# Attention stage of a hybrid diffusion step: one of two GpSimd folds taken out, VectorE adds both halves, and ScalarE writes the first copy of the running sum

## The reference, cut to what matters

```python
def one_block(qi):
    s = jnp.einsum('bqhgd,bkhd->bhgqk', qi.astype(F32), k.astype(F32))
    p = jax.nn.softmax(s, axis=-1)
    return jnp.einsum('bhgqk,bkhd->bqhgd', p, v.astype(F32))
```

## Time and profile before

| | |
|---|---|
| median of 3 runs | 3383.89 us (3378.5 to 3384.28) |
| profiled execution, its own time | 3377.92 us |
| its span, first to last instruction | 3376.2 us |
| attention stage in it (exponentials) | 282.4 to 1079.8 us |
| mean granted TensorE clock | 0.971 of full speed |

### The profile page before, as it was taken

How to read it: one execution, slowest core, us unless ns; L and a number is a source line. 1 busy time by engine, 2 the same in 40 slices (tenths; PEclk the granted TensorE clock), 3 DMA queues, 4 the chain that set the end, 5 groups by cost and what they waited for, 6 DMA issues and landing times. The chain is left out here.

```text
span 3376.2 us, 48426 instructions
## 1 busy us (share of the span) xinstructions
PE 3177.5 (94%) x18066; PEld 2778.3 (82%) x18066; DVE 2378.0 (70%) x3262; ACT 1713.6 (51%) x2475; POOL 1710.5 (51%) x910
## 2 busy tenths in 40 slices
PE   6988999999998799998899699999999999899998
PEld 5975777777776797887688699999999999688886
DVE  4877999999996575339633588988888987222367
ACT  5865888888887685221244433344444333211122
POOL 2655999999997011111023377756766774000001
PEclk8998999999998899999999899999999999899999
DMA  6432011111100444338575567757785775555466
GB/s 217 156 121 76 28 49 45 51 44 47 49 21 24 141 154 144 109 97 260 174 226 183 184 202 229 238 163 245 230 246 156 225 221 158 191 200 183 175 254 224
DMA packets 431529, 518.42 MB, mean 154 GB/s; under 512 B 40112, under 2 KB 322048, under 8 KB 431296
## 3 DMA queue, kind: packets, MB, share of 16 engines
q1 hardware_dynamic: 384224, 412.21, 38.4%
q10 hardware_dynamic: 43968, 91.86, 7.9%
q0 software_dynamic: 3104, 11.27, 0.8%
HBM read 341.62 MB, written 173.64 MB: 153 GB/s over the span
## 5 line engine op out<-in xcount | busy, mean ns | idle before, releaser
L781 POOL TENSOR_TENSOR att_tlo<-att_prob,att_thi 128x1024 fp32r<-128x1024 f32 x292 | 694.0, 2405 | 62.7 <-ACT att_thi L950 62.7
L166 PE MATMUL fu_p<-fu_hhi,fu_whi 128*128 128x384 f32 x1848 | 619.5, 335 | 28.5 <-PEq L111 18.5
L168 PE MATMUL fu_p<-fu_hhi,fu_wlo 128*128 128x384 f32 x1848 | 618.6, 335 | 0.0
L167 PE MATMUL fu_p<-fu_hlo,fu_whi 128*128 128x384 f32 x1848 | 618.5, 335 | 0.0
L945 ACT ACTIVATE att_prob<-att_p_s 128x512 f32<-128x512 f32 x584 | 341.4, 592 | 86.7 <-PE att_p_s L841 80.8
L166 PEld LDWEIGHTS fu_p<-fu_hhi,fu_whi 128*128 128x128 f32 x1848 | 348.0, 188 | 31.5 <-issue 18.8
L993 DVE TENSOR_REDUCE att_mx<-att_p_r 128x1 f32<-128x512 f32 x512 | 341.4, 683 | 44.4 <-PE att_p_r L805 43.3
L167 PEld LDWEIGHTS fu_p<-fu_hlo,fu_whi 128*128 128x128 f32 x1848 | 347.9, 188 | 0.0
L168 PEld LDWEIGHTS fu_p<-fu_hhi,fu_wlo 128*128 128x128 f32 x1848 | 347.8, 188 | 0.0
L950 ACT ACTIVATE att_thi<-att_prob 128x1024 fp32r<-128x1024 f32 x292 | 309.8, 1061 | 9.3
L1807 POOL TENSOR_TENSOR fu_wsum<-fu_ws 128x1024 f32<-128x1024 f32 x66 | 178.7, 2708 | 233.9 <-DMA fu_ws<-in_w_ffn_dram 124.1
(11 more groups left out here) (361 smaller groups left out, 8045.0 us busy)
## 6 DMA issues: line engine op xcount, KB each, us to landing
fu_ws<-in_w_ffn_dram SPq DMA_DIRECT2D x132, 512.0 KB, 8.3
gated_d<-fu_out SPq DMA_DIRECT2D x99, 448.0 KB, 5.8
fd_src<-gated_d SPq DMA_DIRECT2D x63, 704.0 KB, 4.2
second_d<-fu_hs ACTq DMA_DIRECT2D x77, 512.0 KB, 3.3
fu_hs<-in_w_ffn_dram ACTq DMA_DIRECT2D x121, 256.0 KB, 4.2
fd_second<-second_d SPq DMA_DIRECT2D x40, 512.0 KB, 5.9
fd_w<-second_d SPq DMA_DIRECT2D x37, 512.0 KB, 5.3
ga_h<-hT_d SPq DMA_DIRECT2D x36, 512.0 KB, 4.2
```

What stands on the lines that cost most here:

```text
L166: pe.matmul(out, ah, bh, start=first, stop=False)
L167: pe.matmul(out, ah, bl, start=False, stop=False)
L168: return pe.matmul(out, al, bh, start=False, stop=last)
L781: pool.tensor_tensor(tlo[:, sl, :], prob[:, sl, :], thi[:, sl, :].bitcast(F32), ALU.subtract).then_inc(s.lo, 1)
```

## The change

Step 6 leaves the list of folded steps. POOL has one fold less in each latent unit, and DVE adds both halves of step 6. The copy of the first half into `p_sum` goes from DVE to ACT, in step 1, right behind ACT's copy of the finished sum; it waits for that copy (`sums_out`), and DVE's next addition waits for it (`s.sum`).

```diff
     AHEAD = 2
-    FOLDED = (2, 6)
+    FOLDED = (2,)
...
                         act.activation(sums[:, b.kv, :], p_sum[:, :], ACT.Copy).then_inc(s.sums_out, 1)
+                    if S.sum and S.sum[1] == 0:
+                        b, j = S.sum
+                        act.wait_ge(s.ex, b.g0 * 2 + 1)
+                        wait(act, s.sums_out, b.n)
+                        act.activation(p_sum[:, :], prob[:, b.step_no[0] % SLOTS_P, 0:ROW], ACT.Copy).then_inc(s.sum, 1)
                     if S.fin:
...
-                    if i == 0 and j == 0:
-                        wait(dve, s.sums_out, b.n)
-                        dve.tensor_copy(p_sum[:, :], half).then_inc(s.sum, 1)
-                    else:
-                        dve.wait_ge(s.sum, done)
-                        dve.tensor_tensor(p_sum[:, :], p_sum[:, :], half, ALU.add).then_inc(s.sum, 1)
+                    dve.wait_ge(s.sum, done)
+                    dve.tensor_tensor(p_sum[:, :], p_sum[:, :], half, ALU.add).then_inc(s.sum, 1)
...
                         for i in range(1 if b.nds > 1 and j in FOLDED else 2):
-                            add(b, j, i)
+                            if i or j:
+                                add(b, j, i)
                             if pieces:
                                 piece(*pieces.pop(0))
```

## The result

The changed kernel takes 3397.21 us (median of 12 runs, 3391.79 to 3404.0), the one before 3382.89 us (12 runs, 3376.32 to 3390.19). The ratio is 1.0049, with a 95% interval of 1.0041 to 1.0057: slower by half a per cent, with POOL relieved of a fold in each unit. The profiled execution has a span of 3390.0 us against 3376.2.

A forecast was written before the change was run, and what follows sets the result against it. The bound was taken to be a ring of waits, PE, ACT up to `osb`, DVE, PE, not full POOL. 31 x 0.41 = 12.7 us plus 0.3 us made 13.0 us, so about 3397 us; range 3383 to 3406.

The forecast's parts named there:

- the ring PE, ACT up to `osb`, DVE, PE: Attention stage: three engines carry each unit in turn, each waiting for the one before; POOL is full but bounds nobody.
- both gates: Values DVE's long stretch needs, `osb` and the fold of step 2; forecast 0.35 us late by `osb`, 0.41 with the fold.
- The fold taken from POOL: Step 6: frees 1.26 us of POOL a unit, worth 0 on the ring; bounds 0 and 1.26 us.
- the rival that POOL is the bound: Whole stage: it would lose what POOL loses, 32 x 1.26 = 40 us, giving 3344 us; chance 12%.
- The copy taken from DVE in step 1: Step 1 on DVE: frees 0.60 us, worth 0 as the next maximum waits for PE anyway; bounds 0 and 0.60.
- The third addition of step 6: Three DVE additions in a row: next maximum 0.08 us late, covered by idle time, cost 0; uncovered 0.80 us a unit.
- The copy on ACT: Step 1 on ACT: delays the exponentials, `osb` and the fold, so DVE's long stretch starts 0.41 us late each unit.
- The second gate: Fold of step 2, late through `thi` of step 1: raises the delay of DVE's long stretch from 0.35 to 0.41 us.
- The sum: 31 latent units x 0.41 = 12.7 us, with 0.3 us for the first and prompt units: 13.0 us, about 3397 us.
- The prompt part: The four prompt units, priced together with the first unit: 0.3 us for the copy's move, bounds 0 and 3 us.
- the short wait for the fold: Sign in the changed profile: the reader of the fold in step 2 may show a short wait for POOL.
- The sign for the third addition: Sign in the changed profile: maximum behind the three additions comes no later from the unit's first score than before.

The follow-up runs named there:

- e1: Kernel before with only the fold of step 6 taken out, the first copy staying on DVE: 3378.2 us, ratio 0.999.
- e2: Changed kernel with both folds kept (steps 2 and 6), so only the copy moves from DVE to ACT: 3401.55 us, ratio 1.0059.
- e3: Kernel before with ACT's `osb` moved in front of `thi` of step 2: 3373.93 us, ratio 0.9984 to before.
- e4: Changed kernel with ACT's `osb` moved in front of `thi` of step 2: 3394.52 us, ratio 1.0041 to before.
- e9: Changed kernel with one DVE maximum ahead of the addition of the fold, `osb` left behind `thi`: 3395.9 us, ratio 1.0048 to before.
- e6: Kernel before with `osb` early, one DVE maximum ahead of the fold's addition, and step 6 unfolded: 3355.1 us, ratio 0.992.
- e5: Kernel before with `osb` early and one DVE maximum ahead of the fold's addition, both folds kept: 3361.5 us, ratio 0.9942.
- e8: Kernel before with a third fold on POOL, in step 4: 3416.67 us, ratio 1.0103.
- e7: Changed kernel with `osb` early and one DVE maximum ahead of the fold's addition: 3375.47 us, ratio 0.9982 to before.

## Why the prediction was right

*The bound.* The reading that POOL's 98% bounds nobody, and that the ring PE, ACT up to `osb`, DVE, PE does, was right for the latent units but the last: e1 shows the first half, e2, e3, e4 and e9 the second. One wait was left out of the ring: PE's piece also waits for the reciprocal behind `osb` (in 400 to 1000 us 22.1 us at its weight load, 11.9 before). It does not set the pace, since in e4 it is gone and the unit is the same. The rule of highest occupancy (the Trainium skill, "Perfetto Trace Analysis", "Identifying the Most-Contended Engine") named POOL. e1 does not bear that out in 30 of the 32 latent units; at the end of the stage the fold less gave 3 us of the 40 that the rule would have made of it. With both gates open, e6 against e5, it gave 0.21 us a unit, a sixth of the 1.26 us.

*The fold taken from POOL*, put at 0: 0 in each of the 30 units (24.38 us in e1), but 1.55 us less in the last latent unit and 1.55 us less in the first prompt unit, where the prediction had not looked. There the rival that POOL is the bound had a point.

*The copy taken from DVE in step 1*, put at 0: the maximum behind it still waits for PE (0.47 us idle in the changed kernel where the copy stood), and DVE's idle time before L1040 grew. This agrees, though no run takes the copy from DVE and leaves ACT as it was.

*The third addition of step 6*, put at 0.08 us late and covered: 0.02 us late in e1. Right.

*The copy on ACT*, the term that counted, was right in its path and too small in size. I had it start 0.61 us behind the copy of `sums` and hold the next for 0.48; it started 0.67 us behind (883.99 to 884.66) and held it for 0.54 (to 885.20), 0.06 us more at each end. The exponentials of step 1 come 0.74 us late instead of 0.61, `osb` 0.47 instead of 0.35, the fold's addition 0.51 instead of 0.41, and the unit is 0.53 us longer instead of 0.41. The second gate, the fold, is real: in the changed kernel it adds about 0.05 us (the addition starts 0.15 us behind the reciprocal's start, 0.10 before) to 0.08 us (e9), where 0.06 had been put (0.41 - 0.35).

*The sum.* 30 units gave 15.9 us where 31 x 0.41 = 12.7 had been put. The last latent unit gave 0.95 us back, for which the prediction had nothing: the copy alone makes it 0.56 us longer (e2, 25.01 us), the fold less alone 1.55 us shorter (e1). The prompt part, from its first score to the end of the stage, took 0.3 us more (33.58 to 33.88), as put, but by luck: 2.47 us more in e2 and 1.55 us less in e1. The profiled execution starts the stage's scores 2.2 us earlier than the one of before and spends 2.3 us more on the first unit (28.15 against 25.85). e8, which has neither half of the change, has a first unit of 28.19 us too, and e9, which has both, one of 26.49, so this is not the change's. In the end 3397.21 us against 3397, with the medians 14.3 us apart and the ratio at 16.6 us (0.0049 x 3383): 13.0 us had been put for what measured 14.3 to 16.6. The agreement to the microsecond is luck: the 30 units were priced 3.2 us too low in all and the copy at the end of the stage too low as well, the fold's 3 us there were left out, and the median of before fell by 1.0 us with more runs (3383.89 to 3382.89).

*The signs.* DVE's idle time before L1040, 1 us or more: 1.15. The wait in step 2 on ACT gone: yes. POOL's share down by 5 points: 6.8, and its waits for `thi` more and longer (84 instead of 37, up to 1.5 us instead of 0.3). A wait for the copy itself at DVE's addition, which would have spoken against the prediction, is not in the list of 400 to 1000 us; nor is the short wait for the fold that I had thought possible. The sign for the third addition was badly put: I wrote that the maximum behind it would come no later from the first score, but it lies behind the delayed stretch and comes 23.47 us after it (904.03 - 880.56) instead of 22.91. That is the unit's own 0.53 us, as e1 shows by its absence.

## What to carry to other kernels

Before moving work off a full engine, look for who waits for it: here an engine that was 98% busy with an empty list of waiters had nothing to sell in the units where the list was empty, and 3 us where it was not, at the end of the stage. With nearly the same share it held others up once something else was opened or added. When work is moved instead, its price is not the instruction's length but what stands behind it in its new queue; here 0.6 us on an engine with 12% idle time cost 0.53 us a unit, because the idle time lay elsewhere. And where a value is late, ask for a second one behind the same delay: moving `osb` alone gained nothing in the changed kernel, and opening the fold's gate as well gained 19 us (e4 to e7).

## What was not expected of the hardware

The two copies on ACT, by the tile `att_p_sum` of the changed kernel, 400 to 1000 us (count, shortest, median and longest in ns):

```profile
L925 ACT ACTIVATE att_sums<-att_p_sum x24: 577/579/583, 410.2 to 983.7; 128x512 f32<-128x512 f32 x24
L930 ACT ACTIVATE att_p_sum<-att_prob x24: 602/603/604, 410.8 to 984.3; 128x512 f32<-128x512 f32 x24
```

From SBUF to PSUM ACT takes 0.603 us, from PSUM to SBUF 0.579; I had taken the second's row for the first. An ACT instruction that waits for the one right before it started 0.09 us after that one's end here (884.57 to 884.66, and 0.089 to 0.093 us in all 35 such pairs of the trace), three times the 0.03 us that I had read behind the exponentials.
